# Five reorderings on three engines of a float32 four-stage transformer kernel on one core

## The reference

```
h = h + ssd_mixer(rmsnorm(h))           # 8 groups of 4 heads, state 128, chunks of 128, both directions
    z, xbc, dt = split(u @ w_in)
    xbc = silu(dwconv(xbc, 5 taps))      # -> x (heads), B, C
    y = ssd_scan(x, dt, B, C) + reversed scan + x * d_skip
    y = rmsnorm(y * silu(z), per group) ; return y @ w_out
h = h + gla_mixer(rmsnorm(h))           # 4 heads, both directions
h = rmsnorm(h)                          # end of the first block
u = rms_norm(h)
proj = u @ w_in                         # -> conv_in, c_q, c_kv, k_rope_raw, gates
k_rope = apply_rope(k_rope_raw, cos, sin)
h = h + (gates0 * conv(conv_in) + gates1 * attention(c_q, c_kv, k_rope)) @ w_out
h = h + cross_attention(rms_norm(h), mem)
h = h + square(relu(rms_norm(h) @ w1)) @ w2 ; return rms_norm(h)
```

## Time and profile before

| | |
|---|---|
| median of 3 runs | 1791.13 us (1789.34 to 1793.04) |
| profiled execution | 1790.72 us, of which the span of the profile is 1789.0 us |
| TensorE busy | 1688.9 us, 94% of the span |
| DVE / ACT / POOL busy | 1127.9 / 841.1 / 367.2 us |
| mean granted TensorE clock | 0.981 of full speed |
| chain that ended last | TensorE 71%, DVE 14%, ACT 6%, issue 4% |
| SSD stage / GLA stage / second block | to about 550 / to about 979 / to the end |

### The profile page before, as it was taken

One profiled execution on the slowest core, in us unless ns is written; L12 is line 12 of the kernel. 1 busy time (PEld: TensorE's weight loads), 2 busy tenths in 40 slices (PEclk: granted clock), 3 DMA queues, 4 the chain that ended last, 5 costly groups with the idle time before them and its releaser, 6 DMA issues.

```text
span 1789.0 us, 20987 instructions
## 1 busy us (share of the span) xinstructions
PE 1688.9 (94%) x7944; PEld 1359.6 (76%) x7944; DVE 1127.9 (63%) x1520; ACT 841.1 (47%) x1365; POOL 367.2 (21%) x299
## 2 busy tenths in 40 slices
PE   6888999999989999999988899999899899999998
PEld 4766778777767788787866678887688688888886
DVE  6677777887777575756567767776556553434343
ACT  5656656656624354435354434447354442323232
POOL 0354554445531000000006112230220200000001
PEclk9889999999999999999999999999999999999999
DMA  3633444344312222222222232232233233333332
GB/s 106 182 113 112 131 126 133 118 142 124 89 44 81 57 71 71 78 76 71 60 83 65 71 80 67 60 81 92 74 91 103 86 95 95 95 96 104 95 95 71
DMA packets 260107, 164.58 MB, mean 92 GB/s; under 512 B 26910, under 2 KB 249287, under 8 KB 258983
## 3 DMA queue, kind: packets, MB, share of 16 engines
q1 hardware_dynamic: 260006, 163.25, 31.8%
HBM read 160.86 MB, written 2.36 MB: 91 GB/s over the span
## 4 chain that ended last, share of the span: by engine, by line
PE 71%; DVE 14%; ACT 6%; issue 4%; POOL 2%; DMA 2%; SPq 0%; DVEq 0%; ACTq 0%; POOLq 0%
PE stream L79 20%; PE stream L81 19%; PE stream L80 19%; DVE weights_lo L147 2%; DVE ssd_x L995 2%; ACT weights_hi L137 1%; PE q L1977 1%; PE q L2001 1%; PE q L79 1%; PE q L788 1%; PE q L81 1%; PE q L80 1%; POOL h_sum_of_squares L220 1%; DVE ssd_m L1073 1%; PE q L817 1%
## 5 line engine op out<-in xcount | busy, mean ns | idle before, releaser
L79 PE MATMUL stream<-u_lo,weights_hi 128*128 128x512 f32 (+2 forms) x1312 | 532.7, 406 | 11.7 <-DVE u_lo L249 4.5
L81 PE MATMUL stream<-u_hi,weights_hi 128*128 128x512 f32 (+2 forms) x1312 | 515.7, 393 | 0.0
L80 PE MATMUL stream<-u_hi,weights_lo 128*128 128x512 f32 (+2 forms) x1312 | 515.4, 393 | 0.0
L147 DVE TENSOR_TENSOR weights_lo<-weights_raw,weights_hi 128x1024 fp32r<-128x1024 f32 (+4 forms) x269 | 330.4, 1229 | 281.0 <-ACT weights_hi L137 280.8
L137 ACT ACTIVATE weights_hi<-weights_raw 128x1024 fp32r<-128x1024 f32 (+4 forms) x269 | 268.6, 1000 | 458.4 <-PE stream L81 431.2
L79 PEld LDWEIGHTS stream<-u_lo,weights_hi 128*128 128x128 f32 (+2 forms) x1312 | 248.7, 190 | 77.8 <-issue 9.7
L80 PEld LDWEIGHTS stream<-u_hi,weights_lo 128*128 128x128 f32 (+2 forms) x1312 | 248.3, 189 | 54.8 <-issue 4.9
L81 PEld LDWEIGHTS stream<-u_hi,weights_hi 128*128 128x128 f32 (+2 forms) x1312 | 247.5, 189 | 55.3 <-issue 0.5
L217 POOL COPY h_sum_of_squares<-h_squares 128x512 f32<-128x512 f32 x5 | 3.2, 649 | 790.9 <-ACT h_squares L205 790.9
L79 PE MATMUL stream<-mlp_a_lo,weights_hi 128*128 128x512 f32 x256 | 100.2, 391 | 0.0
L81 PE MATMUL stream<-mlp_a_hi,weights_hi 128*128 128x512 f32 x256 | 99.7, 389 | 0.0
(11 more groups left out here) (468 smaller groups left out, 2891.1 us busy)
## 6 DMA issues: line engine op xcount, KB each, us to landing
weights_raw<-in_w_mlp_dram SPq DMA_DIRECT2D x64, 512.0 KB, 3.8
weights_raw<-in_ssd_w_in_dram SPq DMA_DIRECT2D x48, 512.0 KB, 4.1
weights_raw<-in_gla_w_in_dram SPq DMA_DIRECT2D x40, 512.0 KB, 3.8
ssd_cum_steps<-ssd_cum_rows SPq DMA_DIRECT2D x32, 512.0 KB, 5.0
weights_raw<-in_w_in_dram SPq DMA_DIRECT2D x29, 512.0 KB, 3.8
ssd_exp_cum<-ssd_cum_pairs SPq DMA_DIRECT2D x16, 512.0 KB, 7.6
weights_raw<-in_ssd_w_out_dram SPq DMA_DIRECT2D x16, 512.0 KB, 3.6
weights_raw<-in_gla_w_out_dram SPq DMA_DIRECT2D x13, 512.0 KB, 3.4
```

What stands on the lines that cost most here:

```text
L79: pe.matmul(out, lh, rl, start=first, stop=False, skip_group_check=skip)
L80: pe.matmul(out, ll, rh, start=False, stop=False, skip_group_check=skip)
L81: return pe.matmul(out, lh, rh, start=False, stop=last, skip_group_check=skip)
L147: dve.tensor_tensor(lo, raw_view(c, n), hi.bitcast(F32), ALU.subtract).then_inc(c.w_split, 1)
```

## The change

Instructions keep their kind, operands and number; five groups of them stand at another place in their engine's order. Nothing changes on POOL and SP.

1. TensorE, round 1 of the SSD stage: the second z unit is streamed before the transposes of slot 0.
2. DVE, slot 7 of rounds 1 and 2: `assemble(g, 0)` is issued before the other taps of C. The condition `(i, k) not in SSD_OUT` leaves rounds 3 to 7 as they were, and in round 8 nothing stands between the two places.
3. DVE, last round of the SSD stage: the closes of tiles 1 to 3 of each output unit stand before its four rests; before, the rests stood between them.
4. DVE, projection stage, slot 6: the rotary keys stand before the unit's rest (L147) instead of behind it.
5. ACT, end of the GLA stage: both u_hi of an output unit (L243) stand before its four squares; before, u_hi and two squares followed tile by tile.

```diff
@@ TensorE, SSD stage, slot 0
                 if k == 0:
+                    if g == 0:
+                        stream_products(c, pe, unit_in(1, 1), lambda j: c.uh[:, j, :], lambda j: c.ul[:, j, :])
                     pe.wait_ge(s_silu, g + 1)
@@ DVE, SSD stage
                 pi, pk = before(i, k)
+                alone = k == 7 and g in G and (i, k) not in SSD_OUT
+                if alone:
+                    assemble(g, 0)
                 if pi in G and pk in CONV:
...
                     for j in range(1, 4):
                         close(pi, pk, j)
-                        if of == SG - 1:
-                            scale_rest(c, dve, nx, half * 4 + j - 1)
                     if of == SG - 1:
-                        scale_rest(c, dve, nx, half * 4 + 3)
+                        for j in range(4):
+                            scale_rest(c, dve, nx, half * 4 + j)
...
-                if k == 7 and g in G:
+                if k == 7 and g in G and not alone:
                     assemble(g, 0)
@@ ACT, end of the GLA stage
                     for m in range(m0, m0 + tiles):
+                        scale_tile(c, act, nx, m, free_value(c, out_tile(GH - 1, m)))
+                    for m in range(m0, m0 + tiles):
                         final = free_value(c, out_tile(GH - 1, m))
-                        scale_tile(c, act, nx, m, final)
                         square_tile(c, act, m, final)
                         square_tile(c, act, m, final, gain)
@@ DVE, projection stage
+                if k == 6:
+                    dve.wait_ge(s_ta, 1)
+                    dve.tensor_scalar(tbl[:, :], tbl[:, :], cst[:, 2:3], None, ALU.mult).then_inc(s_tb, 1)
...
+                    dve.tensor_scalar(tbl[:, :], tbl[:, :], float(QN + QR) ** -0.5, None, ALU.mult)\
+                       .then_inc(s_tb, 1)
                 if k < N:
                     split_lo(c, dve, n0 + k + 2)
```

More of the change, by code:

```diff
@@ L1813, in _ @@
                        .then_inc(c.bank_free[t % SB], 1)
+                if k == 6:
+                    dve.wait_ge(s_ta, 1)
+                    dve.tensor_scalar(tbl[:, :], tbl[:, :], cst[:, 2:3], None, ALU.mult).then_inc(s_tb, 1)
+                    dve.wait_ge(s_tb, 12)
+                    dve.wait_ge(c.tile_done, t + 1)
+                    dve.tensor_tensor(krt[:, :], bank(c, t)[:, :], tbl[:, :], ALU.mult)\
+                       .then_inc(c.bank_free[t % SB], 1)
+                    dve.wait_ge(*free_value(c, t))
+                    dve.tensor_tensor(krt[:, :], krt[:, :], c.rstd, ALU.mult).then_inc(s_tb, 1)
+                    dve.tensor_scalar(tbl[:, :], tbl[:, :], float(QN + QR) ** -0.5, None, ALU.mult)\
+                       .then_inc(s_tb, 1)
                 if k < N:
```

11 lines of the change are left out of this document (removed).

## The result

| | before | after |
|---|---|---|
| median | 1791.13 us (1789.34 to 1793.04) | 1798.63 us (1797.52 to 1799.63) |
| ratio | | 1.0042, 95% interval 1.0028 to 1.0057 |
| span of the profiled execution | 1789.0 us | 1796.4 us |
| TensorE busy | 1688.9 us | 1689.5 us |

The kernel became slower by 7.5 us (5.0 to 10.2), where +5.3 was forecast. TensorE does the same work in nearly the same busy time, so what was added is mostly time in which it waits.

The account below looks back on a forecast made before the run. TensorE, busy 94% of the span, was taken as the bound, through idle, lower clock and waits. Terms -0.1 + 4.5 + 1.7 - 0.9 + 0.1 = +5.3 us on 1791.1 gave 1796.4 us; 8-in-10 range 1788.5 to 1800.5.

Parts of the forecast that it names:

- the slow clock at the transposes of rounds 2 and 3: TensorE, SSD stage: a longer idle stretch puts the lower clock on the transposes, costing 2.5 us in each round.
- the first centre tap of round 1: SSD round 1: expected as before; coming 3 or more us earlier at the round's end would show the forecast wrong.
- Rival A: Round 1: the stall at 69.97 really holds the round, in full -8.2 us there, total 1788.3 us; chance 0.10.
- The first centre tap of round 2: SSD round 2: forecast wrong if this tap does not come 1 to 2 us later.
- 2.5 us for each restart: Transposes of rounds 2 and 3: mean loss at the lower clock behind TensorE's idle, from 2.8, 3.0 and 1.6.
- Rival B: Rounds 2, 3 and slot 8: clock does not fall or recovers before it matters; -1.4 us, 1789.7; chance 0.14.
- Rival C: ACT's and DVE's queues set the round's end, taking up about half the sums-of-y cost; 1793.5 us; chance 0.14.
- 1.3 at the first wait: Last SSD round, TensorE's wait at 535.33: moved rests add 2 x 0.65 us; 2.8 if each takes 1.39.
- 0.4 at the next stage: First product of the stage after SSD: it waits for the second unit's four rests, +0.4 us (0 to 0.7).
- one add's remainder once: Rests beside POOL's adds: the shared port lock costs one add's remainder once, then rests run at own speed, giving 1.3.
- The new idle: Projection stage: TensorE idle from 1022.5 to 1025.4, 2.9 us, with 1.7 us lost to the lower clock behind it.
- POOL loses that if it can't catch up, while the rests come by as much earlier: End of GLA: one u_hi (0.6) ahead of the first square delays POOL; value +0.1 us, bounds -0.1 and +0.6.

Follow-up runs that it names:

- z_first_alone: Kernel before with only z's second unit streamed ahead of the transposes in round 1; ratio 0.9999, -0.2 us.
- sums_first_alone: Kernel before with only the sums of y issued ahead of C's taps in rounds 1 and 2; ratio 1.0030, +5.4 us.
- sums_first_filled: Kernel before with sums of y ahead of C's taps, plus 30 and 22 unread TensorE products before the transposes of rounds 2 and 3; ratio 1.0006, +1.1 us.

## Why the prediction was right

The mechanism held in its main step, the slow clock at the transposes of rounds 2 and 3, and each part went the way that was forecast; the sum was 2.2 us too low (5.3 against 7.5).

- **Edit 1**, forecast -0.1: -0.2. The wait went to xw on DVE at 83.65; the text had it ended by DVE or ACT before 85, and L1073 where it was. Not as foreseen, the first centre tap of round 1 comes 2.1 us earlier (ACT at 83.98 in place of 86.04), of which 0.5 is left at the second tap (91.86, 92.40) and nothing at the third (101.39, 101.20). Rival A falls with z_first_alone.
- **Edit 2**, forecast +4.5: +5.4 and +5.7. The forecast's points in order: x6 near 110.7 (111.14), idle 8.6 us (8.32), transposes at 125.7 (125.88), x8 at about 2 us (1.94), idle of some 7 us in round 3 (6.70), clock 0.5 behind both. The first centre tap of round 2 comes 2.1 us later (143.57, 141.46), where 1 to 2 was forecast. The clock was forecast at 2.5 us for each restart, 5.0 for both; by the table above it was 4.5 in after and 4.2 in sums_first_alone, so no term is shown to be too low. The rounds say the same: 84.97 us less the middle of the seven kernels with the order of before (80.3 to 81.4, middle 80.9) is 4.1, 85.37 is 4.5. What the timed 5.4 and 5.7 have beyond that is not placed; their intervals hold the 4.5. Rival B (no clock lost) is excluded by the 0.50 in the window; what it describes is sums_first_filled, +1.1 us. Rival C (the queues of ACT and DVE take up half) is excluded by the same table: the loss came through in full.
- **Edit 3**, forecast +1.7 as 1.3 at the first wait and 0.4 at the next stage: +1.8 timed, 1.8 by the narrower distance. The parts of it were sized wrongly and made up for each other. The four rests took 4.80 us, 1.20 each on average, not 0.65, so L147 starts 5.34 us behind the last close (538.73 less 533.39), 3.30 before (532.38 less 529.08): 2.0 later, not 1.3. One by one they take 0.74, 1.78, 1.77 and 0.74 (at 534.00, 534.66, 536.37, 538.06): two of them begin while an add of POOL's runs, which ends at 535.90 and at 537.59. The prediction had one add's remainder once; but POOL's next add stands 0.14 us behind, and it was paid twice. Against that, L147 took 1.21 us and not the 2.30 that it took beside POOL's adds, and the wait grew by 0.94 only. The second place cost 0.62 where 0.4 was forecast: 1.6 for both.
- **Edit 4**, forecast -0.9: -1.3 timed, -1.2 by distance. The new idle is 2.63 us where 2.9 was worked out, and the lower clock behind it took part of the gain.
- **Edit 5**, forecast +0.1 with +0.6 as its upper bound: 1.0 by distance, +1.3 timed. Here a step failed, "POOL loses that if it can't catch up, while the rests come by as much earlier": the value of +0.1 took it that POOL catches up. It did not. Its first copy comes 0.6 us later behind the close, and its row of copies and sums takes 0.4 more (26.57 against 26.15), which is the 1.0. What makes the row longer is not shown. The instruction that reads the last sum waits for POOL (5.40 us, 3.99 before), so POOL's sums are the path and the rests are not.

About 0.5 us of the 7.5 is not placed (7.0 from the parts), less than any interval here. Of the 2.2 us by which the forecast was low, edit 5 is 0.9 to 1.2; the rest is the unplaced part of edit 2's timed value and this 0.5, less the 0.3 to 0.4 that edit 4 gained beyond its forecast, and no step of the forecast is shown to be behind it. The two profiled executions differ by 7.4 us, but not all of that is the change: from the 98th to the 120th L147, where nothing was edited, before took 150.05 us and after 151.65, and other kernels with the same code up to 153.93. The agreement of 7.4 and 7.5 is in part chance.

## What to carry to other kernels

An idle stretch of TensorE can cost twice, by its length and by the lower clock behind it, and each price is paid only if what pays it is on the path: both were free in edit 1, the second cost 4.2 to 4.5 us in edit 2. Before a stall is shortened by running later work earlier, look at what then stands behind the idle time: here a state product and a unit with time to spare had stood there, and had shielded the transposes on the path. Work moved into the gap keeps the clock up if little idle time is left ahead of the next instruction on the path (0.9 to 1.7 us in sums_first_filled), and it is worth what the next engine in line allows, not its length.
